# Transformer step with a routed expert layer: the first product of a pair of experts cut around the turning of its rows, the next rows turned in two halves, row copies on VectorE, and one ScalarE table during the experts

## What is computed

```python
def moe_swiglu(h, w_router, wg, wu, wd):
    logits = (h @ w_router).astype(jnp.float32)
    top_v, top_i = lax.top_k(logits, TOP_K)
    top_p = jax.nn.softmax(top_v, axis=-1)
    gates = jnp.sum(jax.nn.one_hot(top_i, N_EXPERTS, dtype=jnp.float32) * top_p[..., None], axis=-2)
    act = jax.nn.silu(jnp.einsum('bnd,edf->bnef', h, wg)) * jnp.einsum('bnd,edf->bnef', h, wu)
    act = act * gates.astype(h.dtype)[..., None]
    return jnp.einsum('bnef,efd->bnd', act, wd)
```

## Time and profile before

| | us |
|---|---|
| median of 3 runs | 1716.21 |
| lowest and highest | 1714.31, 1717.48 |
| span of the profiled execution | 1715.0 |

### The profile page before, as it was taken

The page is one execution under the profiler, slowest core; times in us unless marked ns, Lnnn a source line. Parts: engine busy times, 40 slices in busy tenths (PEclk is TensorE's granted clock), DMA queues, the critical chain, the costliest instruction groups (busy, mean ns, idle before and its releaser), DMA issues. The chain is left out here.

```text
span 1715.0 us, 24854 instructions
## 1 busy us (share of the span) xinstructions
PE 1557.4 (91%) x9206; PEld 1035.1 (60%) x9207; DVE 756.4 (44%) x1225; ACT 575.5 (34%) x980; POOL 88.8 (5%) x109
## 2 busy tenths in 40 slices
PE   4798989999999799899787999989999799999795
PEld 1684567788888486467523565645555477777432
DVE  0483776433332654675601443434345433333325
ACT  0432554333331442450202443443344432332201
POOL 2010002200000010000100000000000000000002
PEclk8899999999999899999799999989999899999997
DMA  9244535943441634541999999999999477787993
GB/s 344 101 147 163 197 123 188 350 143 111 148 147 50 221 123 139 195 148 45 403 391 379 378 389 393 387 343 379 377 394 376 166 291 264 265 294 264 363 365 137
DMA packets 206623, 432.19 MB, mean 252 GB/s; under 512 B 11880, under 2 KB 52840, under 8 KB 206224
## 3 DMA queue, kind: packets, MB, share of 16 engines
q1 hardware_dynamic: 195712, 390.64, 62.7%
q0 software_dynamic: 7712, 29.05, 4.7%
q10 hardware_dynamic: 3056, 10.62, 1.8%
HBM read 409.55 MB, written 20.71 MB: 251 GB/s over the span
## 5 line engine op out<-in xcount | busy, mean ns | idle before, releaser
L2048 PE MATMUL ps<-d_ring_parts,scratch_parts 128*128 128x512 f32 (+1 forms) x444 | 171.9, 387 | 14.0 <-DVE hT_parts L1335 9.2
L2443 PE MATMUL ps<-ring,hT 128*64 128x512 f32 (+1 forms) x512 | 113.1, 585 | 20.7 <-DMA ring<-in_w_moe_up 11.1
L2048 PE MATMUL ps<-gu_ring_parts,scratch_parts 128*128 128x512 f32 (+1 forms) x336 | 128.5, 383 | 0.0
L2449 PE MATMUL ps<-ring,hT 128*32 128x256 f32 x1760 | 119.9, 389 | 8.4 <-DMA ring<-in_w_moe_up 6.9
L1873 DVE TENSOR_TENSOR cst<-cst,ps 128x256 f32<-128x256 f32 (+2 forms) x89 | 32.8, 368 | 198.0 <-ACT cst L1160 198.0
L2048 PE MATMUL ps<-d_ring_parts,hT_parts 128*128 128x512 f32 (+1 forms) x312 | 119.2, 382 | 0.0
L1185 ACT ACTIVATE qkv_parts<-ring 128x1024 fp32r<-128x1024 f32 x102 | 103.1, 1049 | 13.2 <-issue 13.2
L2048 PEld LDWEIGHTS ps<-d_ring_parts,scratch_parts 128*128 128x128 f32 x444 | 84.7, 191 | 32.3 <-issue 9.3
L2048 PE MATMUL ps<-gu_ring_parts,o_parts 128*128 128x512 f32 x264 | 103.2, 391 | 0.0
L2449 PEld LDWEIGHTS ps<-ring,hT 128*32 128x32 f32 x1760 | 55.9, 111 | 59.5 <-issue 16.6
L1168 ACT ACTIVATE cst<-ps 128x128 f32<-128x128 f32 (+1 forms) x51 | 16.1, 315 | 225.0 <-PE ps L2465 215.7
(11 more groups left out here) (398 smaller groups left out, 3204.5 us busy)
## 6 DMA issues: line engine op xcount, KB each, us to landing
ring<-in_w_moe_gate SPq DMA_DIRECT2D x176, 512.0 KB, 9.9
ring<-in_w_moe_up SPq DMA_DIRECT2D x176, 512.0 KB, 11.3
ring<-in_w_moe_down SPq DMA_DIRECT2D x176, 512.0 KB, 10.0
gu_ring<-in_w_ada SPq DMA_DIRECT2D x48, 1024.0 KB, 7.4
gu_ring<-in_w_in SPq DMA_DIRECT2D x16, 1024.0 KB, 7.4
gu_ring<-in_w_ffn_gate SPq DMA_DIRECT2D x11, 1024.0 KB, 5.5
gu_ring<-in_w_ffn_up SPq DMA_DIRECT2D x11, 1024.0 KB, 8.1
d_ring<-in_w_ffn_down SPq DMA_DIRECT2D x11, 1024.0 KB, 10.0
```

What stands on the lines that cost most here:

```text
L2048: ins = pe.matmul(out, a, w, start=(start and n == 0), stop=(stop and n == 2))
L2443: ins = pe.matmul(ps[64 * j:64 * j + 64, bank, 0:2 * f].rearrange("p (a f) -> p a f", a=2), hT[:, kc, col:col + 64], wt[:, :, f * j:f * j ...
L2449: ins = pe.matmul(ps[32 * j:32 * j + 32, bank, 0:FC].rearrange("p (a f) -> p a f", a=2), hT[:, kc, col:col + 32], wt[:, :, P * j:P * j + P ...
```

## The change

Four edits, all at the passages:

1. **First product in two halves.** `first_step` does the matmuls of the first four slices of `hT` (the base rows are there) before it waits for `y_act` and `y_dve`, then turns the other rows, then does the last four.
2. **Half of the base rows turned early.** At the end of a body, four of the eight transposes of the next base rows go in front of the wait for the hidden block's parts, into the bank that is free. `turned_rest` of the last step is moved on VectorE in front of the last `split_low`.
3. **VectorE copies rows.** VectorE copies all four banks of the turned rows; ScalarE copies none. ScalarE makes the high part of `hT` in two instructions of 128 columns, one ahead of the first silu and one behind it. `rest_act` is gone, and `hT_hi_ready` for turns that don't make it is raised at the end of a body.
4. **One table kept.** A silu of one column of `lam_exp`, a value that is no longer used, stands before the loop.

```diff
+                if turns > (ng > 0):
+                    act.wait_ge(hidT_mm, s0 + turns * STEPS).then_inc(hT_hi_ready, turns - (ng > 0))
...
                 with act.If(variant > 1):
-                    act.wait_ge(rest_turned, t + 1)
-                    for q in range(2):
-                        ins = act.activation(hT[:, 0:4, P + P * q:2 * P + P * q],
-                                             ps[:, 2 * q, :].rearrange("p (k t) -> p k t", k=4), ACT.Copy)
-                    ins.then_inc(rest_act, 1)
                     act.wait_ge(base_act, t + 1)
                     act.wait_ge(base_dve, t + 1)
-                    act.wait_ge(rest_act, t + 1)
-                    act.wait_ge(rest_dve, t + 1)
-                    act.activation(hT_hi, hT[:, :, 0:2 * P], ACT.Copy).then_inc(hT_hi_ready, 1)
+                    act.activation(hT_hi[:, :, 0:P], hT[:, :, 0:P], ACT.Copy)
                     act.wait_ge(gu_mm, t * STEPS + (DENSE + 1))
                     act.activation(hid_e[:, 0, 0:FC], ps[:, 6, 0:FC], ACT.Silu).then_inc(sil_ready, 1)
-
+                    act.wait_ge(rest_dve, t + 1)
+                    act.activation(hT_hi[:, :, P:2 * P], hT[:, :, P:2 * P], ACT.Copy).then_inc(hT_hi_ready, 1)
+
+            act.activation(lam_exp[:, 0:1], lam_exp[:, 0:1], ACT.Silu)
...
-                    for i in ahead[len(early):]:
+                    late = ahead[len(early):]
+                    for i in late[:1]:
+                        split_low(i)
+                    if k == len(steps) - 1 and k in in_parts:
+                        turned_rest(k)
+                    for i in late[1:]:
                         split_low(i)
...
                     dve.wait_ge(rest_turned, t + 1)
-                    for q in range(2):
-                        ins = dve.tensor_copy(hT[:, 4:8, P + P * q:2 * P + P * q],
-                                              ps[:, 2 * q + 1, :].rearrange("p (k t) -> p k t", k=4))
+                    for q in range(4):
+                        c = P + P * (q // 2)
+                        ins = dve.tensor_copy(hT[:, 4 * (q % 2):4 * (q % 2) + 4, c:c + P],
+                                              ps[:, q, :].rearrange("p (k t) -> p k t", k=4))
...
+            def turn_half_rows(i, half):
+
+                for q in range(4):
+                    kc = 4 * half + q
+                    ins = pe.transpose(ps[:, 6 + half, P * q:P * q + P], x[:, i, P * kc:P * kc + P], ident)
+                return ins
...
+                def hidden_copied():
+
+                    pe.wait_ge(hidT_copied, s0 + turns * STEPS)
+                    if len(steps) - 1 in in_parts:
+                        pe.wait_ge(hidT_rest, DENSE + (t + turns) * RESTS)
+
                 def turn_next(n):
 
                     pe.wait_ge(rows_landed, (n + 1) * (16 * LOADS))
-                    turn_rows(0, (6, 7)).then_inc(base_turned, 1)
+                    spare = len(steps) % 2
+                    turn_half_rows(0, spare)
+                    hidden_copied()
+                    turn_half_rows(0, 1 - spare).then_inc(base_turned, 1)
...
                 with pe.If(variant > 1):
-                    pe.wait_ge(y_act, t * HELD + HELD)
-                    pe.wait_ge(y_dve, t * HELD + HELD)
-                    pe.wait_ge(rows_landed, t * (16 * LOADS) + 16 * LOADS)
-                    turn_rows(1, (0, 1))
-                    turn_rows(2, (2, 3)).then_inc(rest_turned, 1)
                     pe.wait_ge(base_act, t + 1)
                     pe.wait_ge(base_dve, t + 1)
                     for kc in range(KD):
+                        if kc == KD // 2:
+                            pe.wait_ge(y_act, t * HELD + HELD)
+                            pe.wait_ge(y_dve, t * HELD + HELD)
+                            pe.wait_ge(rows_landed, t * (16 * LOADS) + 16 * LOADS)
+                            turn_rows(1, (0, 1))
+                            turn_rows(2, (2, 3)).then_inc(rest_turned, 1)
```

18 lines of the change are left out of this document (3 added, 15 removed).

## The result

| | before | after |
|---|---|---|
| median, us (8 runs each, beside each other) | 1716.85 | 1710.38 |
| lowest and highest, us | 1714.31, 1720.07 | 1706.63, 1712.01 |
| span of the profiled execution, us | 1715.0 | 1708.5 |
| PE busy, us | 1557.4 | 1548.9 |
| ACT busy, us | 575.5 | 555.6 |

The ratio is 0.9948, with a 95% interval of 0.9933 to 0.9963: 8.9 us less (6.4 to 11.5), where the forecast was 14.9. The kernel is faster, as foretold, and 40% of the gain is missing. By the ratio the changed kernel stands at 1707.3 us against the 1716.21 of the prediction, inside the range; its own median stands 0.9 us above the upper end.

What follows compares the result with a forecast made beforehand. TensorE's gains at passages 2, 3 and 4 were taken to move everything behind, while pair 1 is bound by transfers. 7.9 + 6.6 + 0.4 = 14.9 us took the span from 1715.0 to 1700.1, median 1701.3; range 1698.5 to 1709.5.

Steps and rivals of the forecast that it cites:

- pair 2 belongs to the transfers: Rival, chance 0.10: TensorE catches up with the transfers in pair 2, passage 2 gives nothing; 7.0 us gained, 1709.2 us.
- The end belongs to the transfers: Rival, chance 0.07: last expert's loads are limited from before passage 4 on, so nothing comes of the gain; about 1716 us.
- the signs named: Expected after the change, among others: passage 3 about 8 us earlier, passage 4 about 14.5, granted clock 1.0 throughout.
- The way over the branches: TensorE's idle time at the loop top ahead of the first product: taken as 1.33 us, 2.36 kept for the range.
- the clock rival: Rival, chance 0.20: remaining idle times keep TensorE's clock low, 5.6 us go; 9.3 us gained, 1706.9 us.
- Gain at passage 2: 7.9 us: Passage 2: the first product ends at 1131.9 instead of 1139.8 us, counted as a gain of 7.9 us.
- The slower rival: Rival, chance 0.06: entering code beside full transfers stops TensorE 5.24 us at loop top and body, both passages; 1722.3 us.
- It reached the top at 1342.16, 5.4 us after VectorE's last result copy, loaded a table: Passage 3: ScalarE's loop-top arrival before the change; the same 5.4 us put its new arrival at 1339.2 us.
- the rival with VectorE: Rival, no chance of its own: VectorE's four copies come 1 us later, TensorE waits 0.6 and 0.3 us; inside the range.
- 6.6: Passage 3: gain of 4.6 us up to the product's end plus 2.0 us from the vanished wait behind the silu.
- Passage 4: 0.4 foretold: Passage 4: no weight part stands ahead of the low part, so only the four early transposes gain, 0.4 us.

Runs made afterwards that it cites:

- the version with the small variants first: The changed kernel with TensorE testing for the two small-expert variants ahead of the large one at the loop top: 1718.52 us, ratio 0.9984.
- the run with two copies: The changed kernel with two of VectorE's four copies of the turned next rows left out, so its output differs: 1706.73 us in one run.

## Why the prediction was right, and where its size failed

**What bounds it: right.** Gains of passages 2, 3 and 4 move all behind them, and what lies ahead of passage 2 belongs to the transfers. Between passages 2 and 3 the stretch stayed at 185.6 to 186.1 us in nearly all kernels, so the rival "pair 2 belongs to the transfers" didn't come (the two others, 187.4 and 187.6, had matmuls of step 1 at the lower clock). "The end belongs to the transfers" didn't come either, but is not wholly away: TensorE waits for weights in the last expert in every trace, 5.4 us before and 6.1 after (3.4 to 6.8 in all).

**The range held in part by luck.** It was widened for the clock and for the transfers of pair 2, and neither came; three losses outside both (the stop at the body, ScalarE's arrival, the end) took their place. Of the signs named, passage 3 began 5.4 us earlier by the two traces (about 8 foretold) and passage 4 10.6 us (about 14.5).

**The passages up to the product's end: right to 0.3 us.** From the start of P2 and of P3 to the end of the product I had 1131.9 - 1116.3 = 15.6 us at passage 2 and 1341.2 - 1325.9 = 15.3 at passage 3; measured 15.4 (1132.98 - 1117.61) and 15.6 (1336.10 - 1320.54). The way over the branches was 1.30 and 1.74 us where I had 1.33. "Control Flow Timing" of "Advanced Engine Details and Errata" in the Trainium skill had given 1.3 as an estimate; passage 2 agrees, passage 3 is 0.4 us above. It fails at the version with the small variants first, where two more compares would be 0.2 us, an estimate by the page, and the stop grew by 3.2 to 3.7. The clock came back in full, so the clock rival didn't come.

**The body's entry: wrong by 1.9 us.** "Gain at passage 2: 7.9 us" stops at the product's end and takes step 1 to follow at once. Measured 6.1: the stop of 1.94 us. I had asked of the top of the loop what its branches cost once less work covers them, and had not asked the same of the body: before, all sixteen matmuls lay behind the last wait that held TensorE, now eight. At passage 2 the packet of code that stands ahead of the body started at about the same time in both traces (1132.8 before, 1132.1 after); before, the product ran on until 1139.76 and covered it. The slower rival named such stops, at 5.24 us each, and was dismissed with passage 1, whose row shows the loop top and not the body.

**ScalarE's arrival: wrong by 2.8 us.** "It reached the top at 1342.16, 5.4 us after VectorE's last result copy, loaded a table" took the load's start as the arrival. The load ran inside the way; the arrival is 8.2 us behind that copy. The silu thus came at 1337.38 instead of 1336.1, and the first down product 4.9 us behind the product's end instead of 4.1. VectorE's way of 4.48 instead of 3.72 us put the end of its copies at passage 2 at 1133.13, just behind the product's end, as the rival with VectorE had it; the run with two copies shows that it cost nothing. Passage 3 to 4 gave 5.3 us for 6.6.

**Passage 4: 0.4 foretold, -0.2 measured.** The wait ahead of the second four transposes fell from 1.39 to 0.63, and the stop ahead of the small first product rose by 0.8. It ends 2.3 us after a packet of code has landed in both traces (1611.1 to 1613.38, 1600.7 to 1602.99), so by these rows what TensorE saves ahead of it goes into the stop.

**The end: not in the sum, 3.9 us.** I costed what TensorE gains as moving everything behind it, and looked for other bounds only among the transfers of weights. A second chain runs there, GpSimd's gathers and VectorE's folds in one buffer, which ended 1.1 us ahead of TensorE's transposes before (1688.56, against 1689.68). But VectorE makes the picks in between (0.86 us, to 1689.54), so only 0.1 us was slack. The chain begins with the last expert, so it moved by 10.9 us along with TensorE, but it came out 2.9 us longer, by its fifth link: gather to fold took 7.1 to 7.7 us in the traces of one buffer with a wait of 0.6 us or less, and 10.3 to 12.7 in the five with more. That chain varies: the wait for the picks was 0, 0.6, 0.8, 3.2, 4.8, 5.2 or 5.5 us in traces of kernels with the change. And behind the longer stop of 3.0 to 3.3 us the small product ran at full clock in some traces and not in others.

The sum with what was measured: 14.9 - 1.8 (P2) - 1.3 (P3 to P4) + 0.5 (between them) - 0.6 (passage 4) - 3.9 (end) = 7.8 us.

**The shares: partly wrong.** I had given most of the gain to the split product. Alone it gives nothing that can be told from no change, since ScalarE's copies and the lower clock take the place of the wait; the earlier low part and the four transposes, which I had costed at 1.0 + 0.4 us and the clock, give 7.1 us alone by the trace.

## What to carry to other kernels

When a wait is taken away, list every other engine's arrival at that place, copies as well as results, and measure it from the last thing that engine did before the branches, never from the first instruction shown behind them. A sequencer's way through branches is free only as long as queued work covers it: here half the work behind the last wait that holds it brought a stop of 1.94 us. Ahead of counting a gain to the end, find the second chain that ends there and its slack, with the work between its end and the need taken off.
